# Splitting the mixer weights of a decoder layer on ScalarE and VectorE, without GpSimd

## The reference

```python
proj = rmsnorm(h, g_mix) @ w_in
q, k, v, u_pool, q_mem, gate_logits = jnp.split(proj, SPLITS, axis=-1)
...
merged = g[:,:,0] * y_attn + g[:,:,1] * y_pool + g[:,:,2] * y_mem   # g = sigmoid(gate_logits + b_gates)
h = h + merged @ w_out
h = h + moe(rmsnorm(h, g_ffn), w_router, b_router, w_gate, b_gate, w_up, b_up, w_down, b_down)
```

## Time and profile before

| what | value |
|---|---|
| time, median of 3 runs | 1363.21 us (1360.21 to 1363.3) |
| span of the profiled execution | 1359.7 us |
| mixer stage | 0 to 414.9 us |
| expert stage, 16 pairs of experts | from 414.9 us |
| TensorE busy (share of the span) | 1212.4 us (89%) |
| VectorE busy | 524.0 us (39%) |
| ScalarE busy | 211.6 us (16%) |
| GpSimd busy | 223.5 us (16%) |

### The profile page before, as it was taken

The page is one execution under the profiler, slowest core; times in us unless marked ns, Lnnn a source line. Parts: engine busy times, 40 slices in busy tenths (PEclk is TensorE's granted clock), DMA queues, the critical chain, the costliest instruction groups (busy, mean ns, idle before and its releaser), DMA issues.

```text
span 1359.7 us, 14264 instructions
## 1 busy us (share of the span) xinstructions
PE 1212.4 (89%) x5572; PEld 594.3 (44%) x5572; DVE 524.0 (39%) x776; ACT 211.6 (16%) x356; POOL 223.5 (16%) x71
## 2 busy tenths in 40 slices
PE   5988587967798999999999999999999999999998
PEld 4777465745674333243333333334333333333332
DVE  6689879898734121212212122121212212122122
ACT  4433422211101001000110100011010010001000
POOL 3885545447610000000000000000000000000000
PEclk9998799978998999999999999999999999999999
DMA  8553343426467978999999999999999999999994
GB/s 275 191 186 114 103 155 111 142 88 248 178 255 295 420 329 371 430 427 428 429 428 428 428 428 429 427 429 429 428 429 428 428 428 429 428 429 427 429 428 185
DMA packets 59452, 458.66 MB, mean 337 GB/s; under 512 B 9249, under 2 KB 9889, under 8 KB 34849
## 3 DMA queue, kind: packets, MB, share of 16 engines
q1 hardware_dynamic: 57136, 454.31, 81.0%
q0 software_dynamic: 1104, 3.93, 0.9%
q10 hardware_dynamic: 1184, 0.07, 0.1%
HBM read 457.24 MB, written 1.05 MB: 337 GB/s over the span
## 4 chain that ended last, share of the span: by engine, by line
PE 71%; DVE 21%; issue 4%; ACT 3%; DMA 1%; POOL 1%; DVEq 0%; ACTq 0%; POOLq 0%
PE bank L1486 33%; PE bank L1539 17%; PE bank L1244 7%; PE bank L1491 5%; PE bank L1506 5%; PE bank L1473 3%; DVE stat L987 2%; ACT region L740 1%; DVE ring_split L770 1%; DVE prob L990 1%; DVE region L856 1%; PE bank L1213 1%; DVE ring_split L783 1%; DVE stat L763 1%; DVE region L1167 1%
## 5 line engine op out<-in xcount | busy, mean ns | idle before, releaser
L1486 PE MATMUL bank<-experts_ring,region 128*64 128x512 f32 x2048 | 453.6, 595 | 14.2 <-DVE region L1176 14.2
L1486 PEld LDWEIGHTS bank<-experts_ring,region 128*64 128x64 f32 x2048 | 145.5, 137 | 307.8 <-issue 307.8
L1539 PE MATMUL bank<-experts_ring,region 128*64 128x512 f32 x1024 | 226.8, 595 | 25.1 <-ACT region L740 25.1
L1244 PE MATMUL bank<-ring_split,region_split 128*128 128x512 f32 x768 | 237.8, 411 | 12.5 <-DVE ring_split L775 6.5
L463 POOL TENSOR_TENSOR ring_split<-ring,ring_split 128x2048 fp32r<-128x2048 f32 x42 | 206.9, 4943 | 122.4 <-DVE ring_split L770 84.2
L1244 PEld LDWEIGHTS bank<-ring_split,region_split 128*128 128x128 f32 x768 | 149.6, 199 | 47.6 <-issue 9.5
L1539 PEld LDWEIGHTS bank<-experts_ring,region 128*64 128x64 f32 x1024 | 77.6, 137 | 153.8 <-issue 121.5
L1244 PE MATMUL bank<-ring_split 128*128 128x512 f32 x288 | 115.7, 402 | 0.0
L1198 DVE COPY region<-bank 64x512 f32<-64x512 f32 x32 | 22.2, 694 | 230.5 <-PE bank L1539 230.5
L1181 DVE TENSOR_SCALAR region<-bank 128x512 f32<-128x512 f32 x32 | 22.1, 692 | 229.0 <-PE bank L1491 229.0
L1188 DVE TENSOR_SCALAR region<-bank 128x512 f32<-128x512 f32 x32 | 22.1, 692 | 190.1 <-PE bank L1491 190.1
(11 more groups left out here) (163 smaller groups left out, 740.6 us busy)
## 6 DMA issues: line engine op xcount, KB each, us to landing
experts_ring<-in_w_gate SPq DMA_DIRECT2D x64, 2048.0 KB, 18.9
experts_ring<-in_w_up SPq DMA_DIRECT2D x64, 2048.0 KB, 24.3
experts_ring<-in_w_down SPq DMA_DIRECT2D x64, 2048.0 KB, 28.5
ring<-in_w_in SPq DMA_DIRECT2D x28, 1024.0 KB, 5.2
ring<-in_w_mem_kv SPq DMA_DIRECT2D x4, 1024.0 KB, 9.3
ring<-in_w_b_attn SPq DMA_DIRECT2D x4, 1024.0 KB, 5.0
ring<-in_w_out SPq DMA_DIRECT2D x4, 1024.0 KB, 5.2
region<-in_b_gates POOLq DMA_DIRECT2D x6, 512.0 KB, 5.4
```

Source lines behind the costliest of these rows:

```text
L1244: ins = nc.tensor.matmul(UB[u % 3][:, :], a[:, k, toks], b[:, cols], start=(k == 0 and m == 0), stop=(k == k_n - 1 and m == 2))
L1486: ins = nc.tensor.matmul(dst[h * SLOTS:(h + 1) * SLOTS, :], XE[:, kk, e * SLOTS:(e + 1) * SLOTS], w[:, k, h * HALF:(h + 1) * HALF], start= ...
L1539: ins = nc.tensor.matmul(bank[2][h * SLOTS:(h + 1) * SLOTS, :], AHT[:, k, half * SLOTS:(half + 1) * SLOTS], w[:, k, h * HALF:(h + 1) * HAL ...
```

## The change

GpSimd's 42 subtractions are made by VectorE (`lo_whole`), and the 21 roundings that VectorE made are made by ScalarE (`hi`). GpSimd keeps its roots, tables, clears and transfers, in the same order. The tables `UPPER_AT` and `LOWER_AT` say after which unit ScalarE rounds and VectorE subtracts in the later pieces: a piece n has the subtractions of halves 2n+3 and 2n+4 after its two units on VectorE, and the roundings of halves 2n+4 and 2n+5 on ScalarE. Halves 11 to 18 are subtracted at the end of `norm_rotate(u)` for units 8 to 15, halves 19 to 22 behind the four `mem_scale`. Halves 40 to 43 are rounded one behind the other. In the diff `hi_at` is ScalarE's and the removed `hi` VectorE's.

```diff
+UPPER_AT, LOWER_AT = {}, {}
+for _n in range(len(PIECES)):
+    _second = LAST_UNIT[_n]
+    _first = _second - (2 if PIECES[_n] in ("wbp", "wbm") else 1)
+    for _at, _u, _H in ((UPPER_AT, _first, 2 * _n + 4), (UPPER_AT, _second, 2 * _n + 5),
+                        (LOWER_AT, _first, 2 * _n + 3), (LOWER_AT, _second, 2 * _n + 4)):
+        if _H < 2 * len(PIECES):
+            _at[_u] = _H
...
-            def lower_parts(first, after):
-                for H in range(first, after):
-                    upper_made(pool, H)
-                    nc.gpsimd.tensor_tensor(lower(H), raw(H), upper(H), ALU.subtract).then_inc(lo_ready, 1)
...
+            def hi_at(u):
+                if u in UPPER_AT:
+                    hi(UPPER_AT[u])
...
             qkT(0)
             gate_exp(20)
+            hi_at(20)
             exps(0)
...
                 if h < HEADS - 1:
                     aT(h)
+                hi_at(22 + 2 * h)
                 if h + 2 < HEADS:
                     qkT(h + 2)
...
                 if h < HEADS - 1:
                     o_out(h)
+                hi_at(23 + 2 * h)
             gate_exp(38)
+            hi_at(38)
             for j in range(4):
                 if j == 2:
                     gate_exp(39)
+                    hi_at(39)
...
+            for u in range(40, 44):
+                hi_at(u)
             for j in range(4):
                 act.wait_ge(mgT_done, j + 1)
...
-            def hi(H):
-                dve.wait_ge(raw_in[H % HALVES], 16 * (H // HALVES + 1))
-                nc.vector.tensor_copy(upper(H), raw(H)).then_inc(hi_dve, 1)
+            def lo_whole(H):
+                dve.wait_ge(hi_act, H - EARLY + 1)
+                nc.vector.tensor_tensor(lower(H), raw(H), upper(H), ALU.subtract).then_inc(lo_ready, 1)
...
             turned(1, 1)
+            lo_whole(2)
             turned(1, 2)
             turned(1, 3)
+            lo_whole(3)
             dve.wait_ge(squares, 4)
             mean_square(1, slice(2, 4), D)
+            lo_whole(4)
...
             for n, (rows_, first, col) in enumerate(((KM, 2, 8), (QM, 6, 16))):
+                for H in ((5, 6), (7, 8, 9, 10))[n]:
+                    lo_whole(H)
...
                 nc.vector.tensor_tensor(raw, a, b, ALU.add).then_inc(normed, 1)
+                lo_whole(u + 3)
...
             mem_scale(0)
+            lo_whole(19)
...
             def split_next(u):
-                for H in split_after.get(u, ()):
-                    hi(H)
+                if u in LOWER_AT:
+                    lo_whole(LOWER_AT[u])
...
             mean_square(2, slice(128, 144), P)
-            hi(37)
-            hi(38)
             dve.wait_ge(root_done, 3)
```

More of the change, by code:

```diff
@@ L64 @@
 XLO_SLOT, LO_SLOT = 10, 11
-BY_ACT = 23
 EARLY = 2
@@ L232, in decoder_layer @@
         raw_in = [sem(f"raw_in{i}") for i in range(HALVES)]
-        hi_early, hi_act, hi_dve, lo_ready, lo_early, first_half_used = (sem(n) for n in ("hi_early", "hi_act", "hi_dve", "lo_ready", "lo_early", "first_half_used"))
+        hi_early, hi_act, lo_ready, lo_early, first_half_used = (sem(n) for n in ("hi_early", "hi_act", "lo_ready", "lo_early", "first_half_used"))
         oT_split, mgT_split = sem("oT_split"), sem("mgT_split")
@@ L296, in upper @@
             return half_slot_r[:, HI_SLOT[H % HALVES], :]
[L298 to L302, removed]
         def half_free(engine, H):
@@ L489, in gate_bias @@
                                    .to_broadcast([P, D])).then_inc(gbias_in[n], 16)
-            lower_parts(8, 20)
             pool.wait_ge(kq_done, 4)
@@ L494, in _ @@
             gate_bias(0, "p", D)
-            lower_parts(20, 23)
             pool.wait_ge(mo_done, MHEADS)
             gate_bias(1, "m", 2 * D)
-            lower_parts(23, 30)
             last = UNIT_OF[("wbp", 1, 1)]
@@ L501, in _ @@
             gate_bias(2, "a", 0)
-            lower_parts(30, 37)
             pool.wait_ge(pv_done, HEADS)
@@ L507, in _ @@
             nc.gpsimd.memset(OE, 0.0).then_inc(seed_clear, 1)
-            lower_parts(37, 41)
             pool.wait_ge(merged, 4)
@@ L515, in _ @@
             pool.dma_start(WR, w_router.rearrange("(k p) e -> p k e", p=P)).then_inc(late_in, 16)
-            lower_parts(41, 44)
             root(3, slice(4, 5))
@@ L643, in _ @@
             evac(19, qk_dst(19))
+            hi(23)
             mem_probT(3)
+            def hi_at(u):
+                if u in UPPER_AT:
+                    hi(UPPER_AT[u])
             def qkT(h):
@@ L673, in _ @@
             gate_exp(21)
+            hi_at(21)
             for h in range(HEADS):
@@ L900, in _ @@
             mem_scale(0)
+            lo_whole(19)
             mem_max(1)
             mem_scale(1)
+            lo_whole(20)
             mem_out(0)
@@ L905, in _ @@
             mem_scale(2)
+            lo_whole(21)
             mem_out(1)
@@ L908, in _ @@
             mem_scale(3)
+            lo_whole(22)
             mem_out(2)
@@ L949, in _ @@
             n_merged = [0]
-            split_after = {}
-            for n in range(10, N0):
-                if n == 17:
-                    continue
-                short = PIECES[n] in ("wbp", "wbm")
-                second = LAST_UNIT[n] - (2 if short else 1)
-                for H, u in ((2 * n + 3, second - 1 if short else second), (2 * n + 4, second)):
-                    if H < 2 * N0:
-                        split_after.setdefault(u, []).append(H)
             def split_next(u):
-                for H in split_after.get(u, ()):
-                    hi(H)
+                if u in LOWER_AT:
+                    lo_whole(LOWER_AT[u])
             def unit(u):
```

2 lines of the change are left out of this document (removed).

## The result

| | median | lowest to highest | runs |
|---|---|---|---|
| kernel before | 1361.71 us | 1360.0 to 1363.3 | 4 |
| changed kernel | 1305.09 us | 1302.65 to 1305.79 | 4 |

The ratio is 0.9581, with a 95% interval of 0.9567 to 0.9594: the kernel is 56.6 us faster. The forecast was 1310 us within 1296 to 1332. The profiled execution of the changed kernel has a span of 1303.3 us (forecast 1306.4).

A forecast was written before the change was run, and what follows sets the result against it. It took VectorE, stalled behind GpSimd's subtractions, to bound the heads, with the expert stage moving as a block. Terms -3.2 - 12.9 - 32.8 - 8.9 + 4.5 = -53.3 us gave span 1306.4 and forecast 1310 us, range 1296 to 1332.

The forecast's parts named there:

- start, to unit 8: Units 0 to 7: VectorE's conversion no longer stretched by GpSimd, unit 2 ending at 39.7 instead of 42.9; -3.2 us.
- units 8 to 15, to the last rotation: VectorE's normalise-and-rotate: 35.8 us of stalls go, 18.2 of subtractions and 4.7 of new waits come; -12.9 us.
- to unit 22: Cross-attention: four subtractions, 9.1 us, against stalls of 4.1 and 4.2 us and some smaller ones; 0.
- heads, units 22 to 36: Seven attention heads: 75.4 us instead of 108.2, three at 13.5 each and four with half units 34.9; -32.8 us.
- units 36 to 44: Behind the heads to unit 44: 62.9 us instead of 71.8; -8.9 us.
- TensorE's slower clock after waits: Mixer stage: some ten TensorE waits stay, half of them long, at 0.4 to 1.5 us each; +4.5 us.
- VectorE stood until GpSimd was done: Heads: L987's 4.33 us instruction, against 0.23 when quick, ends as GpSimd's subtraction does; L987's excess is 25.0 us.
- The units behind it run end to end: Start: units following unit 2 run without gaps, so its earlier end carries through; -3.2 us.
- Both new waits: Units 8 to 15, VectorE: 2.0 us for ScalarE's q-memory root, 2.7 for unit 8, earlier covered by stalls.
- Eight subtractions come in, 18.2 us: Units 8 to 15: work added to VectorE before its last rotation ends, 18.2 us.
- The rival in which ScalarE's roundings land on the ring: Heads: ScalarE's roundings delay copies and exponentials, 13 x 1.91 = 24.8 us, time 1335; chance 0.14.
- some 6 more: Ahead of unit 44: without rounding 43 ahead of the merged rows' copies, some 6 us more would go.

The follow-up runs named there:

- roundings_only: Changed kernel with GpSimd's 42 subtractions back in the order of before, all roundings staying on ScalarE; 1336.57 us.
- held_back: Kernel before, with six of GpSimd's subtractions in the heads held until VectorE has done the head's weights, nothing moved to another engine; 1353.05 us.
- root_first: Changed kernel with ScalarE's root of the k-memory rows put ahead of roundings 7 and 8; 1301.65 us.
- late_43: Changed kernel with ScalarE's rounding 43 put behind the four copies of the merged rows; 1301.31 us.
- after_again: The changed kernel itself, unaltered, timed again in the same five rounds as later versions; 1304.89 us.
- extra_reads: Changed kernel with two extra GpSimd subtractions of 128x1024 in each head, whose results nobody reads; 1321.59 us.

## Why the prediction was right, and where it was not

The forecast was 5 us too high: 3.1 us in the span, and the rest because it placed the median 3.5 us above the span, where the profiled execution of the changed kernel lies 2.1 above it. In all runs the time lies 1.8 to 2.4 us above its own span; the 3.5 compared the span of a quicker run with the median of others. The terms, cumulated at TensorE's unit starts (units 8 to 15: at the end of VectorE's last rotation):

| term | predicted | measured |
|---|---|---|
| start, to unit 8 | -3.2 | 0.0 |
| units 8 to 15, to the last rotation | -12.9 | -16.1 |
| to unit 22 | 0 | -0.8 |
| heads, units 22 to 36 | -32.8 | -32.0 |
| units 36 to 44 | -8.9 | -7.7 |
| TensorE's slower clock after waits | +4.5 | within the terms above, some +2.2 of them |
| sum at unit 44 | -53.3 | -56.6 |

*The mechanism* was right, and so were the prices: 2288 ns for 2270, 1910 for 1909, no stretched instruction left. "VectorE stood until GpSimd was done" was read from one pair of rows, and the runs bear it out in four ways: the stall goes with the subtractions, it returns with other GpSimd work, it moves when GpSimd's work moves, and all 36 held instructions of the kernel before end at a fixed distance behind one of GpSimd's. What the prediction did not see is that the excess is not a fixed price per subtraction; roundings_only and held_back, with the same 42, both came out away from the time that was expected of them.

*The start* was wrong. The step that failed is "The units behind it run end to end". They don't. The chain of waits of the changed kernel there:

```profile
43.58 8.68 DMA ring<-in_w_in
...
54.79 1.28 ACT L536
...
56.56 1.23 DVE region L840
57.79 2.21 DVE ring_split L773
...
60.05 2.12 PE bank L1246 x7
```

ScalarE waits for half 8 to land so as to round it, with its root (L536, a table load of 1.28 us ahead of it) queued behind that; VectorE waits 9.3 us for the root; subtraction 7 stands behind the k-memory norm (L840), and unit 6 waits for it in its middle until 60.05. Before, GpSimd had done that subtraction on its own, whatever VectorE waited for. So unit 2 ended 4.8 us earlier (2.0 of it because unit 0 started at 14.08 instead of 16.12, a transfer having landed earlier), and by unit 7 all was lost; in every version without root_first's edit unit 8 starts between 72.6 and 74.7. That is the new wait of an in-order engine that the prediction looked for in the heads and not here; root_first, in which unit 8 starts 4.5 us earlier, shows the cause.

*Units 8 to 15* came out 3.2 us better, which hides that: the last rotation ended at 136.45 us, near the 136 that was forecast, because two errors of 3.2 us cancelled by chance. Both new waits appeared at about their price: VectorE's timeline of the changed kernel has 2.10 us for the root and 3.34 for unit 8 (2.0 and 2.7 forecast).

```profile
75.74 0.20 DVE L768 RECIPROCAL stat<-stat 128x8 f32<-128x8 f32 x1 [2.10 <-ACT stat L536]
75.97 1.22 DVE L840 TENSOR_TENSOR region<-region,stat 128x1024 f32<-128x1024 f32 x1
80.53 0.69 DVE L856 TENSOR_REDUCE stat<-region 128x8 f32<-128x512 f32 x1 [3.34 <-ACT region L522]
...
135.76 0.69 DVE L864 TENSOR_TENSOR region<-tmp 128x512 f32<-128x512 f32 x1
136.37 2.28 DVE L773 TENSOR_TENSOR ring_split<-ring,ring_split 128x2048 fp32r<-128x2048 f32 x1
```

The mis-sized term is the "Eight subtractions come in, 18.2 us": only seven lie ahead of the end of the last rotation, the eighth (136.37) behind it, 2.3 us. The next instruction also starts some 0.08 us before a subtraction's end (84.79 + 2.28 against 86.99), seven times 0.6; and the square of the q-memory rows (L821, now L827), 1.72 us before and 1.22 now, was one more stalled one, 0.5. That makes 3.4.

*The heads* came out at 76.2 us for 75.4. The walk of the queues was right head by head: a pair with two whole units takes 222.13 - 208.69 = 13.4 us (13.5 forecast), those with half units 8.3, 9.5, 8.3 and 9.7 (8.0, 9.4, 8.3 and 9.2). The first matmuls of units 28 and 30 of the changed kernel answer to the earlier trace rows:

```profile
208.69 0.50 PE L1246 MATMUL bank<-ring_split,region_split 128*128 128x512 f32 x1
...
222.13 0.50 PE L1246 MATMUL bank<-ring_split,region_split 128*128 128x512 f32 x1
```

The rival in which ScalarE's roundings land on the ring did not come here: ScalarE is busy 43.1 of 76.2 us. (Its price was counted with 13 roundings in the heads; the trace has ten, 19 us.)

*Units 36 to 44*: the new wait named in the prediction is there, as drawn. The chain of the changed kernel ahead of unit 44:

```profile
304.73 4.89 DMA ring<-in_w_out
...
309.65 1.91 ACT ring_split L531
311.56 0.49 ACT region_split L707
...
313.36 0.61 DVE region L953
...
313.99 0.70 DVE region L958
...
314.72 2.29 DVE ring_split L773
...
317.66 2.50 PE bank L1246 x5
```

Rounding 43 waits for its half to land and the copies wait behind it; from the end of unit 42 to unit 44 it takes 16.6 us (17.3 forecast, 15.9 before). The addition that took 7.86 is L958 here, 0.70. The wait was put at "some 6 more"; late_43 got 3.6 of it back. GpSimd's power took 2.92 us, of the 3.77 of before and the 2.7 taken:

```profile
269.45 2.92 POOL L458 TENSOR_TENSOR stat<-stat,small 128x16 f32<-128x16 f32 x1 [58.92 <-DVE stat L762]
```

*TensorE's clock* was over-priced: "Some ten waits of TensorE stay in the mixer" at 0.4 to 1.5 us. In the heads the granted clock is 0.99 and the stage only 0.8 us longer than walked with quick matmuls. Behind them unit 36 took 6.9 us at a clock of 0.82, where 5.7 was walked (in after_again it took 5.7 at 1.00), and units 40 to 42 took 18.2 us at 0.91, where 17.2 was walked. That is 2.2 us; shorter waits gave 1.0 of it back.

*Not additive.* Of the sum's terms, units 8 to 22 belong to the subtractions alone; the 32 us in the heads were attributed to the end of the stalls, and would have come for the most part by moving VectorE's roundings alone (27 us), or GpSimd's subtractions alone (25 us).

## What to carry to other kernels

Where two engines block each other, the groups by form show it as a mean many times the quickest of the form, and the timeline as ends that agree; the price of an overlap is what is left of the other's instruction, so it depends on who releases whom, and a long instruction that is released right ahead of short, critical ones is the worst case. Such a conflict is ended by taking one engine out, since shifting the long instructions moves the stall to others. When a helper engine's work is put into an in-order queue, every wait ahead of it in that queue becomes its wait: walk that for all stages, the first one too, and put work that waits for a transfer behind work that is ready.

## What was not expected of the hardware

Clears on GpSimd, which read nothing, held VectorE's small one-input instructions (229 to 598 ns) and left its two-input subtractions alone (2288 ns with and without). And the holding goes both ways. The 2934 ns of GpSimd's subtractions of 1024 columns in extra_reads are a mean of two kinds: nine of the sixteen took 2.34 to 2.41 us, four took 4.27 to 4.34. One of the four began at 173.82 us, while a subtraction of VectorE ran from 173.64 to 175.92; it took 4.34 us, so here GpSimd stood for VectorE.
